# The last expert of each group runs last, and the rows of the first thirty tiles are added to the tokens while it runs

## The chip, the cores and the metric

One core of one Trainium2 chip. The metric is the device time of one execution of the whole program, in microseconds; the runs of a kernel are summed up by their median. The profile is of one further execution.

## The reference

One decoder layer over 1024 tokens of width 1024, all in float32: three kinds of attention side by side, an output projection, and then a mixture of experts. Only the mixture and the final norm matter here:

```python
grp = argmax(h @ w_grp + b_grp)                    # one of 4 groups
top_val, top_idx = top_k(expert logits of grp, 2)  # two of its 8 experts
w_top = softmax(top_val) * grp_gate
for e in range(32):
    out += (silu(h @ w_gate[e]) * (h @ w_up[e]) * gate[:, e]) @ w_down[e]
x = x + out
return rmsnorm(x, norm_final)
```

Each token has exactly two experts, both in one group of eight. So no token has two experts with the same place in a group: experts 7, 15, 23 and 31, the last of the four groups, give each token one row or none.

## The kernel before, in words

The engines run five separate programs that meet at semaphores: SyncE (SP) starts the large DMAs, GpSimd (POOL) the gathers by index, ScalarE (ACT) and VectorE (DVE) compute, TensorE (PE) multiplies. `wait_ge(s, v)` stops the engine that meets it, and all that stands behind it in its program, until semaphore `s` has reached `v`.

The attention comes first and ends near 670 us. The output projection writes `x2`, the residual rows of all tokens, 8 tiles of 128 tokens, in SBUF. The router then sorts the 2048 pairs of token and expert into tiles of at most 96 rows (`CAP`): one tile for each of the 32 experts, and two more (`SURE`) for the experts that have more than 96 tokens. The 34 tiles (`NB`) are run in a loop whose body is written out. I count them 0 to 33 in the order in which they run. For tile n:

- SyncE loads the expert's weights, 2 MB and 1 MB, into one of five sets of buffers (`RING`), when tile n-5's down product is done (lines 728 to 734).
- GpSimd gathers the tile's rows of the normalised input from `h2_d` into `XG` (line 897), one tile or two ahead.
- TensorE transposes them (`m_transposes`, L2144), does the product with the gate and up weights (`m_up`, L2153) and the down product (`m_down`, L2161). Its order is: up n, transposes n+1, down n-1.
- VectorE and ScalarE work out the gate (`m_gate`, lines 1704 to 1717: clamp, exponential on ScalarE, add, reciprocal, two products). In the middle of the gate of tile n VectorE copies its half of the transposed rows of tile n+1 (`m_x`, L1696), without which up n+1 can't start.
- Both copy the result from PSUM (`m_out`, L1723), which the next down product needs, and ScalarE stores 96 rows in `Y_d` in HBM (L1163). VectorE's order is: gate n, copy of n-1.

Experts that overflow further go through a loop of 19 trips (`Fori(0, MAX_OVF - SURE)`), which every engine walks after the 34 tiles; each trip asks `If(j < n_ovf)`. With this input `n_ovf` is 0: the bodies are not run, the loop is walked. Its first step is a load of `n_ovf` into a register (`value_load`).

The last stage starts when both of the last stores have landed: GpSimd gathers for each token tile the first and the second expert's rows of its 128 tokens from `Y_d` into `y1` and `y2` (L921, 16 gathers of 512 KB). VectorE adds each, multiplied by its weight, to `x2` (L1775). ScalarE sums the squares (L1193), and in batches (`K_BATCH`) VectorE refines the inverse roots with five small operations (`k_roots`) and does the final product with the gain (`k_final`, L1769), which SyncE stores (L749). Since every slot of `Y_d` could be read, the rows of unused overflow tiles are zeroed earlier, with seven stores during the attention (L658).

Of the kernel before, what the change touches and what calls it, by code (L numbers as in the profile page):

```python
# [24 lines left out]
P = 128  # L25
# [17 lines left out]
NROWS = NTILES * CAP  # L43
# [157 lines left out]
def program(nc, a, out):  # L201
# [5 lines left out]
    with ctx:  # L207
# [99 lines left out]
        zrow = at("zrow", [P, D // 4], f32, ZE + 32 * KB)  # L307
# [24 lines left out]
        slf, shi, slo = (ri(n, [P, 2, NT]) for n in ("slf", "shi", "slo"))  # L332
# [30 lines left out]
        y1 = at("y1", [P, NT, D], f32, ZD)  # L363
        y2 = at("y2", [P, NT, D], f32, ZD + 32 * KB)
        gfin = at("gfin", [P, D], f32, ZC)
# [10 lines left out]
        Y_d = nc.dram_tensor("Y_d", [NROWS, D], f32).ap()  # L376
# [65 lines left out]
        yz_st = sem("yz_st")  # L442
# [43 lines left out]
        ovf_y = sem("ovf_y")  # L486

# [13 lines left out]
        ZERO = 7  # L501
        ROUTES = ((0, 4, "0"), (4, 6, "1"), (6, 8, "2"))
        A_BATCH = ((0, 1), (1, 1), (2, 2), (4, 4))
        K_BATCH = ((0, 3), (3, 3), (6, 1), (7, 1))

        class Events:
# [8 lines left out]
            def did(self, name, ins, eng=None):  # L515
# [3 lines left out]
                if eng is not None:  # L519
# [13 lines left out]
                       "cj", "ej", "ejc", "nov", "info", "ids_ov"])  # L533
# [18 lines left out]
        def _(sp_):  # L552
# [101 lines left out]
            def zero_rows(i):  # L654

                n0, n1 = (NB + (MAX_OVF - SURE) * j // ZERO for j in (i, i + 1))
                sp_.wait_ge(blk_zero, 3)
                sp_.dma_start(Y_d[n0 * CAP:n1 * CAP, :].rearrange("(p r) (q d) -> p (r q) d", p=CAP, q=4),  # L658
                              zrow[0:CAP].unsqueeze(1).broadcast_to([CAP, 4 * (n1 - n0), D // 4])).then_inc(yz_st, 16)

            stored = 0
            for f, x in enumerate(PLAN.full):
# [12 lines left out]
                if f in range(8, 8 + ZERO):  # L675
                    zero_rows(f - 8)
# [26 lines left out]
            sp_.dma_start(wgu[0][:], a["wgu"][0].rearrange("p (k n) -> p k n", k=KC)).then_inc(we_in[0], 16)  # L703

# [26 lines left out]
            for n in range(NE, NB):  # L731
                eid = sp_.value_load(info[0:1, 1 + n - NE:2 + n - NE], min_val=0, max_val=NE - 1)
                sp_.wait_ge(m_dn, n - RING + 1)
                load_expert(eid, n % RING)
# [12 lines left out]
            for t in range(NT):  # L747
                sp_.wait_ge(k_out, t + 1)
                sp_.dma_start(out[t * P:(t + 1) * P, :], y1[:, t, :]).then_inc(k_st, 16)  # L749
# [6 lines left out]
        def _(pool):  # L756
            pool.sem_inc(m_tr, 2)
            nc.gpsimd.memset(ones[:], 1.0).then_inc(blk_zero, 1)
            nc.gpsimd.memset(zrow[:], 0.0).then_inc(blk_zero, 1)
# [30 lines left out]
            pool.wait_ge(blk_zero, 5)  # L790
# [101 lines left out]
            for n in range(NB):  # L892
                p = n % 2
                pool.wait_ge(m_tr, n + 1)
                if n == NE:
                    pool.wait_ge(dve_did, DV.of("ids_ov"))
                pool.indirect_dma_start(  # L897
                    out=XG[0:CAP, p, :], out_offset=None, in_=h2_d,
                    in_offset=bass.IndirectOffsetOnAxis(ap=ids[0:CAP, n:n + 1], axis=0),
                    bounds_check=SEQ - 1, oob_is_err=False).then_inc(xg_in[p], 16)  # L900
            pool.wait_ge(m_tr, 2 + NB)
            n_ovf = pool.value_load(info[0:1, 0:1], min_val=0, max_val=MAX_OVF - SURE)
            with pool.Fori(0, MAX_OVF - SURE) as j:
                with pool.If(j < n_ovf):
# [7 lines left out]
                        bounds_check=SEQ - 1, oob_is_err=False).then_inc(ovf_x, 16)  # L912

            for p in range(2):
                pool.wait_ge(y_st[p], 16 * NB // 2 + 1)
            pool.wait_ge(yz_st, 16 * ZERO)
            pool.wait_ge(ovf_y, 16 * n_ovf + 1)
            apart(pool)
            for t in range(NT):
# [8 lines left out]
        def _(act):  # L928
# [132 lines left out]
            act.wait_ge(blk_zero, 5)  # L1061
# [94 lines left out]
            def m_out(n):  # L1156
# [6 lines left out]
                act.dma_start(Y_d[n * CAP:(n + 1) * CAP, :], YO[0:CAP, p, :]).then_inc(y_st[p], 16)  # L1163
# [9 lines left out]
            act.wait_ge(yz_st, 16 * ZERO)  # L1173
            act.wait_ge(y_st[0], 16 * NB // 2 + 1)
            n_ovf = act.value_load(info[0:1, 0:1], min_val=0, max_val=MAX_OVF - SURE)
            with act.Fori(0, MAX_OVF - SURE) as j:
                with act.If(j < n_ovf):
# [8 lines left out]
                    act.dma_start(Y_d[ts(j + NB, CAP), :], YO[0:CAP, 0, :]).then_inc(ovf_y, 16)  # L1186
# [13 lines left out]
        def _(dve):  # L1200
# [12 lines left out]
            dve.sem_inc(m_y1, 1)  # L1213
            dve.wait_ge(gbc_in, 16)
# [123 lines left out]
            dve.wait_ge(blk_zero, 5)  # L1338
# [385 lines left out]

            m_x(0)
            overflow_ids()
            for n in range(NB):
                m_gate(n)
                if n:
                    m_out(n - 1)  # L1730
            m_out(NB - 1)
            dve.wait_ge(y_st[0], 16 * NB // 2 + 1)
            n_ovf = dve.value_load(info[0:1, 0:1], min_val=0, max_val=MAX_OVF - SURE)
            with dve.Fori(0, MAX_OVF - SURE) as j:
                with dve.If(j < n_ovf):
# [16 lines left out]
                    V_.tensor_copy(out=YO[0:CAP, 0, 512:D], in_=PS[0:CAP, 6, :]).then_inc(ovf_dve, 1)  # L1752

# [14 lines left out]
            def k_final(t):  # L1768
                V_.scalar_tensor_tensor(out=y1[:, t, :], in0=x2[:, t, :], scalar=rstd[:, t:t + 1],  # L1769
                                        in1=gfin[:], op0=ALU.mult, op1=ALU.mult).then_inc(k_out, 1)  # L1770
# [536 lines left out]
```

## Time and profile before

| what | us |
|---|---|
| median of 3 runs | 1215.21 (1213.35 to 1217.25) |
| span of the profiled execution, first to last instruction | 1207.4 |
| TensorE busy | 1099.9 (91% of the span) |
| VectorE busy | 596.5 (49%) |
| ScalarE busy | 381.1 (32%) |
| GpSimd busy | 211.4 (18%) |
| last matmul ends | 1157.5 |

The profiled execution's own time isn't given beside its span; the median of the three runs lies 7.8 us above that span. Times in the profile are from the span's start. A number behind L is the line of the kernel.

### The profile page before, as it was taken

How to read it: one execution, taken by the hardware profiler on the slowest of the kernel's cores; microseconds unless marked ns; L12 is line 12 of the kernel's file. 1: busy time of each engine (PE TensorE's matmuls, PEld its weight loads, DVE VectorE, ACT ScalarE, POOL GpSimd, SP SyncE). 2: the span in 40 equal slices, each digit the busy share in tenths (PEclk: the TensorE clock that was granted, in tenths of full speed). 3: DMA queues.
4: the chain of work that ended last, by engine and by line, in shares of the span. 5: the costliest groups of instructions: out<-in, count | busy, mean ns of one | idle time of the engine just before them, and what ended most of it. 6: DMA issues, size and time to landing. Idle time of an engine off the chain costs nothing.

```text
span 1207.4 us, 29635 instructions
## 1 busy us (share of the span) xinstructions
PE 1099.9 (91%) x12090; PEld 898.5 (74%) x12090; DVE 596.5 (49%) x1584; ACT 381.1 (32%) x693; POOL 211.4 (18%) x460
## 2 busy tenths in 40 slices
PE   6999899999999999999999899959999999999930
PEld 5989788777788888888777688848777777776710
DVE  5341344224666666665685434474443433333338
ACT  6321112221555555544777122200111111111112
POOL 1030000000523332321484000010110000000031
PEclk9999999999999999999999899968999999999975
DMA  9020755371657887863421422169999999999656
GB/s 356 18 87 16 283 162 157 109 222 70 164 134 198 210 217 186 216 144 81 116 58 26 158 97 96 70 221 360 385 380 373 405 376 374 385 384 370 225 179 267
DMA packets 69431, 251.59 MB, mean 208 GB/s; under 512 B 22225, under 2 KB 30321, under 8 KB 59441
## 3 DMA queue, kind: packets, MB, share of 16 engines
q1 hardware_dynamic: 59376, 219.54, 54.3%
q0 software_dynamic: 6112, 16.79, 4.2%
q10 hardware_dynamic: 3808, 13.37, 2.9%
q8 instruction: 98, 1.61, 0.6%
q14 instruction: 37, 0.30, 0.1%
HBM read 205.34 MB, written 49.15 MB: 211 GB/s over the span
## 4 chain that ended last, share of the span: by engine, by line
PE 75%; DMA 10%; DVE 6%; issue 3%; POOL 2%; ACT 1%; SPq 1%; POOLq 0%; DVEq 0%; ACTq 0%
PE PS L2153 13%; PE PS L1829 12%; PE PS L2007 9%; PE PS L2161 8%; PE PS L2089 7%; PE PS L1818 6%; DMA wdn<-in_wdn 5%; PE PS L1985 4%; PE PS L1946 4%; PE PS L1986 3%; PE PS L2144 2%; DMA wst<-in_wt 1%; DMA k<-T_d 1%; PE PS L1864 1%; PE PS L1979 1%
## 5 line engine op out<-in xcount | busy, mean ns | idle before, releaser
L2153 PEld LDWEIGHTS PS<-XT,wgu 128*64 128x64 f32 x4352 | 185.7, 140 | 33.6 <-issue 32.3
L1090 ACT ACTIVATE pt<-PS,cst 128x512 f32<-128x512 f32 (+3 forms) x288 | 167.2, 650 | 108.5 <-PE PS L1986 82.6
L2153 PE MATMUL PS<-XT,wgu 128*64 128x96 f32 x4352 | 192.2, 250 | 7.6 <-issue 5.1
L1398 DVE CUSTOM_DVE_ANT_0 junkm<-PS,cst 128x512 f32<-128x512 f32 (+3 forms) x276 | 133.5, 531 | 77.5 <-PE PS L1946 75.4
L2007 PEld LDWEIGHTS PS<-V,pt 128*64 128x64 f32 x3840 | 121.7, 138 | 22.5 <-issue 10.4
L2007 PE MATMUL PS<-V,pt 128*64 128x65 f32 x3840 | 137.4, 225 | 0.1
L2161 PE MATMUL PS<-wdn,aT 128*96 128x512 f32 x272 | 122.7, 593 | 1.0 <-DVE YO L1723 0.9
L1829 PE MATMUL PS<-hTh,wth 128*128 128x512 f32 x256 | 102.7, 401 | 4.5 <-DVE wtl L1245 4.5
L1829 PE MATMUL PS<-hTh,wtl 128*128 128x512 f32 x256 | 100.6, 393 | 0.0
L1829 PE MATMUL PS<-hTl,wth 128*128 128x512 f32 x256 | 100.3, 392 | 0.0
L1709 DVE TENSOR_SCALAR ge<-PS 128x192 f32<-128x192 f32 x34 | 12.2, 358 | 164.3 <-PE PS L2153 164.3
L823 POOL TENSOR_SCALAR_AFFINE_SELECT pt<-pt 128x128 f32<-128x128 f32 x224 | 64.2, 292 | 163.2 <-ACT pt L1090 120.8
L897 POOL DMA_INDIRECT XG<-h_d,ids x34 | 32.7, 963 | 296.7 <-PE PS L2144 283.2
L2161 PEld LDWEIGHTS PS<-wdn,aT 128*96 128x96 f32 x272 | 41.7, 163 | 56.4 <-issue 56.3
L1946 PE MATMUL PS<-k,q 128*128 128x128 f32 (+3 forms) x324 | 79.9, 348 | 1.6 <-DMA k<-T_d 1.3
L1985 PE MATMUL PS<-q,k 128*128 128x512 f32 (+1 forms) x228 | 81.2, 370 | 0.0
L1986 PE MATMUL PS<-q,k 65*128 65x512 f32 (+1 forms) x240 | 76.4, 339 | 0.0
L1154 ACT ACTIVATE ge<-ge 128x192 f32<-128x192 f32 x34 | 12.3, 363 | 193.1 <-DVE ge L1709 193.1
L1946 PEld LDWEIGHTS PS<-k,q 128*128 128x128 f32 (+1 forms) x324 | 56.7, 191 | 10.1 <-DMA k<-T_d 1.9
L1829 PEld LDWEIGHTS PS<-hTh,wth 128*128 128x128 f32 x256 | 48.5, 190 | 15.7 <-DVE wtl L1245 5.1
L1829 PEld LDWEIGHTS PS<-hTl,wth 128*128 128x128 f32 x256 | 48.5, 190 | 10.8 <-issue 1.0
L988 ACT ACTIVATE thi<-PS,cst 128x512 fp32r<-128x512 f32 x32 | 21.8, 686 | 109.1 <-PE PS L1829 88.5
(275 smaller groups left out, 1654.8 us busy)
## 6 DMA issues: line engine op xcount, KB each, us to landing
wgu<-in_wgu SPq DMA_DIRECT2D x34, 2048.0 KB, 14.0
wdn<-in_wdn SPq DMA_DIRECT2D x34, 1024.0 KB, 23.7
q<-T_d SPq DMA_DIRECT2D x58, 256.0 KB, 4.3
k<-T_d SPq DMA_DIRECT2D x58, 256.0 KB, 5.4
Y_d<-YO ACTq DMA_DIRECT2D x34, 384.0 KB, 10.1
wst<-in_wt SPq DMA_DIRECT2D x16, 512.0 KB, 6.6
T_d<-thi SPq DMA_DIRECT2D x16, 512.0 KB, 2.6
T_d<-tlo SPq DMA_DIRECT2D x16, 512.0 KB, 3.9
```

The lines of the kernel that those rows point to most:

```text
L823: ins = nc.gpsimd.affine_select(out=o, in_=o, compare_op=ALU.is_ge, fill=0.0, base=0, pattern=[[1, P]], channel_multiplier=-1)
L1090: ins = nc.scalar.activation(pt[:, (n + 2) % 6, 0:nt * P], PS[:, n % 3, 0:nt * P], ACT.Exp, scale=C("slopes", h, h + 1), bias=C("kb", w, w ...
L1398: V_.tensor_tensor_reduce(out=junk_[:, 0:L], in0=PS[:, bank, 0:L], in1=tab, scale=1.0, scalar=-3e38, op0=ALU.add, op1=ALU.max, accum_out=m ...
L1818: ins = mm(o, x[:, k, t * P:(t + 1) * P], wv[w][:, k, :], start=(k == 0 and x is hTh and w == 0), stop=(k == KC - 1 and w == 1))
L1829: ins = mm(PS[:, 2 * p + h, :], w[:, p, k * P:(k + 1) * P], x[:, k, h * 512:(h + 1) * 512], start=(k == 0 and w is wth and x is hTh), stop ...
L1946: ins = mm(PS[:, bank, 0:nk * P], q_[:, t * P:(t + 1) * P], k_[:, k0 * P:(k0 + nk) * P], start=True, stop=True)
L1985: mm(o, k1[:, j * P:(j + 1) * P], q1[:, q], start=True, stop=False)
L1986: ins = mm(o, k2[0:HD + 1, j * P:(j + 1) * P], q2[0:HD + 1, q], start=False, stop=True)
L2007: ins = mm(PS[h * HD:(h + 1) * HD, O_BANK[b % 2], (t % 4) * VW:(t % 4 + 1) * VW], pt[0:rows, (n + 2) % 6, q * P + h * HD:q * P + (h + 1) * ...
L2089: ins = mm(PS[:, 2 + h, :], x[:, t % 2, k, :], w[:, k, h * 512:(h + 1) * 512], start=(k == 0 and x is oth and w is woh), stop=(k == KC - 1 ...
L2153: ins = mm(PS[h * HD:(h + 1) * HD, 2 + p, f * CAP:(f + 1) * CAP], wgu[q][:, c, lo:lo + HD], XT[:, p, c, :], start=(c == 0 and f == 0), sto ...
L2161: ins = mm(PS[0:CAP, 5 + h, :], aT[:, p, c, :], wdn[q][:, c, h * 512:(h + 1) * 512], start=(c == 0), stop=(c == 1))
```

## The change

- `TILE` is a new order: the 28 experts that are not the last of their group, the two overflow tiles, and then experts 7, 15, 23 and 31 (`FINAL`). The first thirty tiles (`EARLY`) are stored in `Y_d`, the last four in `Z_d`. SyncE, GpSimd and ScalarE follow this order.
- After the copy of tile 0 VectorE works out, in `last_rows()`, two sets of weights and of slots: `wa`, `slot_a` for rows that lie in the first thirty tiles, `wf`, `slot_f` for the one row of a token that may lie in the last four. A row that isn't in the set has weight 0 and a slot beyond the bounds, which the gather leaves out.
- Behind its last gather for the tiles, GpSimd waits for the stores up to tile 29 and gathers the 16 sets of early rows into twelve buffers `ye`, which lie over the buffers of tile 29's and tile 30's weights.
- VectorE adds them to `x2`: sets 0 to 2 after the copy of tile 30, sets 3 to 10 after the copy of tile 31, sets 11 to 15 after the copy of tile 33. Each add is followed by a wait for its own completion.
- The last stage gathers one set for each token tile, from `Z_d`, and adds it; the roots come in three batches and not four.
- The walk through the overflow loop stays behind the tiles; on SyncE and VectorE it is now also behind the 16 early adds. Its bodies are longer, because an overflow tile is now added to `x2` inside them.
- The zero stores are gone. The final gain is loaded at the end of the attention. Small tiles lie in the part of the constants that is no longer used.

```diff
+FINAL = tuple(range(7, NE, 8))
+TILE = tuple(e for e in range(NE) if e not in FINAL) + tuple(range(NE, NB)) + FINAL
+EARLY = NB - len(FINAL)
+YROWS = EARLY * CAP
+ZROWS = len(FINAL) * CAP
+SKIP = 2.0 ** 16
...
-        K_BATCH = ((0, 3), (3, 3), (6, 1), (7, 1))
+        K_BATCH = ((0, 3), (3, 3), (6, 2))
...
-                if f in range(8, 8 + ZERO):
-                    zero_rows(f - 8)
...
             sp_.dma_start(wgu[0][:], a["wgu"][0].rearrange("p (k n) -> p k n", k=KC)).then_inc(we_in[0], 16)
+            sp_.dma_start(gfin[:], a["g_fin"]).then_inc(gfin_in, 16)
...
-            for n in range(RING, NE):
+            for n in range(RING, NB):
+                e = TILE[n]
+                if e >= NE:
+                    e = sp_.value_load(info[0:1, 1 + e - NE:2 + e - NE], min_val=0, max_val=NE - 1)
                 sp_.wait_ge(m_dn, n - RING + 1)
-                load_expert(n, n % RING)
...
-            sp_.wait_ge(m_dn, NB - (NB - RING) % RING)
-            sp_.dma_start(gfin[:], a["g_fin"]).then_inc(gfin_in, 16)
+                load_expert(e, n % RING)
             sp_.wait_ge(m_dn, NB)
+            sp_.wait_ge(e_add, 2 * NT)
             n_ovf = sp_.value_load(info[0:1, 0:1], min_val=0, max_val=MAX_OVF - SURE)
...
+            pool.wait_ge(dve_did, DV.of("slot_a"))
+            for p in range(2):
+                pool.wait_ge(y_st[p], 16 * EARLY // 2 + 1)
+            for i in range(2 * NT):
+                if i in (0, 6):
+                    pool.wait_ge(m_dn, EARLY + (i > 0))
+                if i >= 12:
+                    pool.wait_ge(e_add, i - 11)
+                pool.indirect_dma_start(
+                    out=ye[i % 12][:], out_offset=None, in_=Y_d,
+                    in_offset=bass.IndirectOffsetOnAxis(ap=slot_a[:, i % 2, i // 2:i // 2 + 1], axis=0),
+                    bounds_check=YROWS - 1, oob_is_err=False).then_inc(ye_in[i % 12], 16)
...
             for t in range(NT):
-                for k, dst in enumerate((y1, y2)):
-                    pool.indirect_dma_start(
-                        out=dst[:, t, :], out_offset=None, in_=Y_d,
-                        in_offset=bass.IndirectOffsetOnAxis(ap=slot[:, k, t:t + 1], axis=0))\
-                        .then_inc(k_in[t], 16)
+                pool.indirect_dma_start(
+                    out=zt[:, t, :], out_offset=None, in_=Z_d,
+                    in_offset=bass.IndirectOffsetOnAxis(ap=slot_f[:, t:t + 1], axis=0),
+                    bounds_check=ZROWS - 1, oob_is_err=False).then_inc(k_in[t], 16)
...
+            def early_rows(*steps):
+
+                for i in steps:
+                    t, k = i // 2, i % 2
+                    dve.wait_ge(ye_in[i % 12], 16 * (i // 12 + 1))
+                    V_.scalar_tensor_tensor(out=x2[:, t, :], in0=ye[i % 12][:], scalar=wa[:, k, t:t + 1],
+                                            in1=x2[:, t, :], op0=ALU.mult, op1=ALU.add).then_inc(e_add, 1)
+                    dve.wait_ge(e_add, i + 1)
+
             m_x(0)
             overflow_ids()
             for n in range(NB):
                 m_gate(n)
                 if n:
                     m_out(n - 1)
+                if n == 1:
+                    last_rows()
+                if n == EARLY + 1:
+                    early_rows(0, 1, 2)
+                if n == EARLY + 2:
+                    early_rows(*range(3, 11))
             m_out(NB - 1)
+            early_rows(*range(11, 16))
             dve.wait_ge(y_st[0], 16 * NB // 2 + 1)
             n_ovf = dve.value_load(info[0:1, 0:1], min_val=0, max_val=MAX_OVF - SURE)
             with dve.Fori(0, MAX_OVF - SURE) as j:
...
+            dve.wait_ge(ovf_add, 15 * n_ovf + 1)
             for t in range(NT):
-                dve.wait_ge(k_in[t], 32)
-                for k, y in enumerate((y1, y2)):
-                    V_.scalar_tensor_tensor(out=x2[:, t, :], in0=y[:, t, :], scalar=w12[:, k, t:t + 1],
-                                            in1=x2[:, t, :], op0=ALU.mult, op1=ALU.add).then_inc((link, k_acc)[k], 1)
-                    if k == 0:
-                        dve.wait_ge(link, lk.next())
+                dve.wait_ge(k_in[t], 16)
+                V_.scalar_tensor_tensor(out=x2[:, t, :], in0=zt[:, t, :], scalar=wf[:, t:t + 1],
+                                        in1=x2[:, t, :], op0=ALU.mult, op1=ALU.add).then_inc(k_acc, 1)
                 if t == 4:
                     k_roots(0)
-                if t >= 4:
-                    for u in ((0, 1), (2,), (), ())[t - 4]:
-                        k_final(u)
+                if t >= 5:
+                    k_final(t - 5)
             k_roots(1)
-            k_final(3)
+            for t in (3, 4, 5):
+                k_final(t)
             k_roots(2)
-            k_final(4)
-            k_roots(3)
-            for t in (5, 6, 7):
+            for t in (6, 7):
                 k_final(t)
```

## Rows read from the trace of the kernel before

**Rows 1.** The page: its span, and the busy time of each engine.
```profile
span 1207.4 us, 29635 instructions
PE 1099.9 (91%) x12090; PEld 898.5 (74%) x12090; DVE 596.5 (49%) x1584; ACT 381.1 (32%) x693; POOL 211.4 (18%) x460
```

**Rows 2.** Stretches: window, busy us (instructions) by engine, clock, DMA share, GB/s.
```profile
900.00:930.00 30.00, 30.00 (x462) 22.50 (x460) 11.49 (x21) 4.34 (x9) 2.87 (x3) 1.00 1.01 369
...
1135.00:1140.00 5.00, 5.00 (x119) 4.88 (x115) 0.28 (x1) 0.00 (x0) 0.00 (x0) 1.00 0.41 138
```

**Rows 3.** Timeline of the last tiles: start, duration, engine, line, operation.
```profile
1121.94 0.96 POOL L897 DMA_INDIRECT XG<-h_d,ids  x1 [8.72 <-PE PS L2144]
...
1125.38 0.32 ACTq L1163 DMA_DIRECT2D Y_d<-YO  x1
...
1139.72 0.36 DVE L1709 TENSOR_SCALAR ge<-PS 128x192 f32<-128x192 f32 x1 [4.75 <-PE PS L2153]
...
1142.19 0.56 DVE L1696 COPY XT<-PS 128x384 f32<-128x384 f32 x1
...
1143.86 5.50 PE L2153 MATMUL PS<-XT,wgu 128*64 128x96 f32 x128
...
1149.40 0.36 DVE L1709 TENSOR_SCALAR ge<-PS 128x192 f32<-128x192 f32 x1 [4.75 <-PE PS L2153]
...
1153.84 3.64 PE L2161 MATMUL PS<-wdn,aT 128*96 128x512 f32 x8 [0.87 <-DVE YO L1723]
...
1157.52 0.69 DVE L1723 COPY YO<-PS 96x512 f32<-96x512 f32 x1 [3.83 <-PE PS L2161]
```

**Rows 4.** The chain of waits: the first two gathers of the tail.
```profile
1162.28 0.96 POOL y L921
...
1163.54 0.94 POOL y L921
```

**Rows 5.** Timeline of VectorE in the tail.
```profile
1169.30 2.60 DVE L1775 SCALAR_TENSOR_TENSOR x<-y,w,x 128x1024 f32<-128x1024 f32 x2 [11.10 <-DMA y<-Y_d,slot]
...
1172.46 7.64 DVE L1775 SCALAR_TENSOR_TENSOR x<-y,w,x 128x1024 f32<-128x1024 f32 x6 [0.56 <-DMA y<-Y_d,slot]
...
1199.54 0.15 DVE L1760 TENSOR_SCALAR nv<-ssq 128x1 f32<-128x1 f32 x1
...
1200.49 3.68 DVE L1769 SCALAR_TENSOR_TENSOR y<-x,rstd,gfin 128x1024 f32<-128x1024 f32 x3
```

**Rows 6.** Stretches, same columns: among the zero stores, and around 670 us.
```profile
460.00:480.00 20.00, 19.72 (x306) 16.67 (x304) 13.32 (x56) 11.34 (x20) 7.63 (x21) 1.00 0.80 213
...
660.00:680.00 20.00, 15.99 (x149) 13.04 (x149) 9.21 (x25) 5.19 (x12) 3.00 (x12) 0.91 0.58 212
```

**Rows 7.** Stretches, columns as in rows 2: two at low clock, one with a gap.
```profile
671.80:675.10 3.30, 3.15 (x10) 2.69 (x11) 2.96 (x9) 0.99 (x3) 0.00 (x0) 0.51 1.10 444
...
826.50:832.00 5.50, 5.46 (x68) 5.49 (x70) 0.55 (x2) 0.00 (x0) 0.00 (x0) 0.50 1.06 382
...
1105.00:1110.00 5.00, 3.59 (x88) 3.40 (x86) 0.00 (x0) 0.00 (x0) 0.00 (x0) 1.00 0.97 356
```

**Rows 8.** DMA issues at 1125.4, 1121.9 and 1162.3 us; last, us to landing.
```profile
Y_d<-YO ACTq DMA_DIRECT2D x1, 384.0 KB, 8.5
...
XG<-h_d,ids POOLq DMA_INDIRECT x1, 9.4
...
y<-Y_d,slot POOLq DMA_INDIRECT x1, 5.2
```

**Rows 9.** Timeline of TensorE: up product 1.
```profile
826.54 8.14 PE L2153 MATMUL PS<-XT,wgu 128*64 128x96 f32 x128 [2.72 <-issue]
```

**Rows 10.** The overflow loop's instructions: count; ns min/median/max; first and last start.
```profile
L1733 DVEq TENSOR_LOAD <-info x1: 543/543/543, 1157.5 to 1157.5; - x1
...
L1734 DVEq COMPARE_BRANCH  x19: 50/56/66, 1158.9 to 1168.5; - x19
...
L2195 PEldq COMPARE_BRANCH  x19: 214/221/3772, 1159.4 to 1176.5; - x19
```

More of the change, by code:

```diff
@@ L361, in program, with late @@
                for q, o in enumerate((ZE, ZD + 16 * KB, ZD + 40 * KB, ZB + 48 * KB, ZC + 16 * KB))]
-        y1 = at("y1", [P, NT, D], f32, ZD)
-        y2 = at("y2", [P, NT, D], f32, ZD + 32 * KB)
-        gfin = at("gfin", [P, D], f32, ZC)
+        zt = at("zt", [P, NT, D], f32, ZD)
+        ye = [at(f"ye{b}", [P, D], f32, (ZC if b < 6 else ZE) + 4 * KB * (b % 6)) for b in range(12)]
+        dead = (4 * COL["dist"][0] + 31) // 32 * 32
+        gfin = at("gfin", [P, D], f32, dead)
+        _do = [dead + 4 * D]
+        def late(name, shape, dt=f32):
+            n = 4
+            for s in shape[1:]:
+                n *= s
+            t = at(name, shape, dt, _do[0])
+            _do[0] += (n + 31) // 32 * 32
+            assert _do[0] <= 4 * COL["distc"][1]
+            return t
+        lm, am, wa, wl, sf, zf, sd, eq, ew, es = (
+            late(n, [P, 2, NT]) for n in ("lm", "am", "wa", "wl", "sf", "zf", "sd", "eq", "ew", "es"))
+        wf, wd, zs, sj = (late(n, [P, NT]) for n in ("wf", "wd", "zs", "sj"))
+        slf, shi = late("slf", [P, 2, NT]), late("shi", [P, 2, NT])
+        slot_a = late("slot_a", [P, 2, NT], u32)
+        slot_f, slot_j = late("slot_f", [P, NT], u32), late("slot_j", [P, NT], u32)
+        jt = late("jt", [P, 1])
         junk3 = at("junk3", [P, D], f32, ZB + 60 * KB)
@@ L486, in program @@
         ovf_y = sem("ovf_y")
+        ovf_g = sem("ovf_g")
+        ovf_add = sem("ovf_add")
+        ye_in = [sem(f"ye_in{b}") for b in range(12)]
+        e_add = sem("e_add")
         k_in = [sem(f"k_in{t}") for t in range(NT)]
@@ L1752, in _ @@
                     V_.tensor_copy(out=YO[0:CAP, 0, 512:D], in_=PS[0:CAP, 6, :]).then_inc(ovf_dve, 1)
+                    dve.wait_ge(ovf_add, 15 * j + 1)
+                    V_.tensor_scalar(out=eq[:], in0=shi[:], scalar1=jt[:, 0:1], scalar2=None, op0=ALU.is_equal)\
+                      .then_inc(ovf_add, 1)
+                    dve.wait_ge(ovf_add, 15 * j + 2)
+                    V_.tensor_scalar(out=jt[:], in0=jt[:], scalar1=1.0, scalar2=None, op0=ALU.add).then_inc(ovf_add, 1)
+                    V_.tensor_tensor(out=ew[:], in0=eq[:], in1=w12[:], op=ALU.mult).then_inc(ovf_add, 1)
+                    V_.tensor_tensor(out=es[:], in0=eq[:], in1=sd[:], op=ALU.mult).then_inc(ovf_add, 1)
+                    dve.wait_ge(ovf_add, 15 * j + 5)
+                    V_.tensor_tensor(out=wd[:], in0=ew[:, 0], in1=ew[:, 1], op=ALU.add).then_inc(ovf_add, 1)
+                    V_.tensor_tensor(out=sj[:], in0=es[:, 0], in1=es[:, 1], op=ALU.add).then_inc(ovf_add, 1)
+                    dve.wait_ge(ovf_add, 15 * j + 7)
+                    V_.tensor_scalar(out=slot_j[:], in0=sj[:], scalar1=SKIP, scalar2=None, op0=ALU.add)\
+                      .then_inc(ovf_add, 1)
+                    dve.wait_ge(ovf_g, 16 * NT * j + 16 * NT)
+                    for t in range(NT):
+                        V_.scalar_tensor_tensor(out=x2[:, t, :], in0=zt[:, t, :], scalar=wd[:, t:t + 1],
+                                                in1=x2[:, t, :], op0=ALU.mult, op1=ALU.add).then_inc(ovf_add, 1)
             dve.wait_ge(gfin_in, 16)
```

94 lines of the change are left out of this document (64 added, 30 removed).

## The prediction

> **What bounds the kernel now.** I read the page first: a span of 1207.4 us with TensorE busy in 91% of it and VectorE in half [rows 1]. The stretches say which stage the change touches. From 830 to 1157 us the 34 expert tiles run; TensorE is busy without a gap and the DMA engines are full too, at 369 GB/s; from 1130 us on the last expert weights drain and the DMA share falls to 0.41 [rows 2]. One tile takes 9.68 us (1139.72 to 1149.40, the gate's first operation in two tiles [rows 3]). In the tail the chain of waits goes from the last copy over its store to GpSimd's gathers, the first at 1162.28 [rows 4], and from 1169.3 VectorE sets the pace: 16 adds and 8 final products of 1.28 us each, with small groups of root operations between [rows 5]. So there are two things to price: what happens from 1125 to 1157 us, where TensorE is the bound, and what VectorE does in series after it. The profiled span is 7.8 us under the median of the runs shown (1215.21); I add the same 7.8 us to the new span.
>
> **Parts that cost nothing.** The seven zero stores leave a stretch where TensorE is busy 19.72 of 20 us and DMA 0.80 of its time [rows 6]; nothing there waits for them: 0, at best the 0.28 us of idle. The load of the final gain moves from 1124.6 us to 670 us, 0.5 MB behind the first expert's weights in a window with a DMA share of 0.58 [rows 6]: 0, up to 2 us if the next load of attention output waits behind it. `last_rows()` adds 22 small operations on VectorE after the copy of tile 0. A small one takes 0.16 us and 0.2 with its link (five in the 0.95 us from 1199.54 to 1200.49 [rows 5]), so 4.4 us; VectorE is idle for 4.75 us before each gate [rows 3], that of tile 2 too. Hidden, by 0.3 us; if not, the gate has 1.1 us in hand (below). The two nearly empty overflow tiles now run 29th and 30th of the 34 and four full experts last: about 0.5 MB of gathered rows moves from the DMA-bound part to behind it. TensorE lost 1.41 us there (busy 3.59 of 5 [rows 7]). I credit 0.5 us (bounds 0 and 1.4).
>
> **The early gathers hold VectorE, and VectorE holds TensorE.** GpSimd starts the 16 early gathers when the store of tile 29 has landed. That store is issued at 1125.38 and takes 8.5 us: 1133.9 [rows 3, 8]. GpSimd needs 0.8 us from a release to its gather (released by the transposes' end at 1121.13, start 1121.94 [rows 3]): 1134.7. The starts are 1.25 us apart (1162.28, 1163.54 [rows 4]); the third is at 1137.2. Landing: 5.2 us on idle DMA engines, 9.4 us among weights [rows 8]; with 0.41 of the DMA time in use [rows 2] I take the middle, 7.3 us: 1144.5. VectorE adds rows 0, 1, 2 between tile 30's copy and tile 32's gate (each add 1.28), so that gate starts at 1145.8 and not at 1139.72: 6.1 us late.
>
> Queued behind it: tile 32's gate contains the copy of tile 33's X. That ended at 1142.75 and its reader, up product 33, started at 1143.86 [rows 3], a slack of 1.1 us. Up product 33 now starts at 1145.8 + 3.0 + 0.15 = 1149.0, 5.1 us late, with TensorE idle in between.
>
> The gate ends at 1145.8 + 3.7 = 1149.5, tile 31's copy adds 0.7: 1150.2. Then eight more adds stand before tile 33's gate; six took 7.64 us [rows 5], eight take 10.2: 1160.4 (their rows are in; the eleventh gather starts at 1147.2). Up product 33 is done by 1157.2 even if it takes 8.14 us [rows 9], so the adds come last. The gate takes 3.2 us without a copy of X, tile 32's copy 0.7, and the last down product waits for that copy, as it does now [rows 3]: start at 1160.4 + 3.2 + 0.7 + 0.15 = 1164.5, where it was 1153.84: 10.7 us late. TensorE has by then been idle for 4 us or more.
>
> **The clock.** After 2.72 us idle TensorE came back at 0.50 (1.2 GHz) and kept it for 5.5 us of work: up product 1 took 8.14 us where up product 33 took 5.50 [rows 3, 7, 9]. Elsewhere the low clock lasted 3.3 us (671.8 to 675.1), and 1.41 us idle cost none [rows 7]. So the last down product, 3.64 us at full clock [rows 3], starts at the low one: 5.3 us if that lasts 3.3, 7.3 if it lasts throughout. I take 6.2: it ends at 1170.7, where it was 1157.5.
>
> **The tail.** Copy 0.7: 1171.4. VectorE adds rows 11 to 15, 5 x 1.28 = 6.4 (their gathers are long in): 1177.8. Now comes what the old profile hides. Each engine loads the number of overflow tiles and walks an empty loop of 19 trips. On VectorE that runs from 1157.5 to 1168.55, 11.05 us [rows 10], beside the store and the first gathers, and its first add came at 1169.3. In the new program each early add ends in a wait that stops the sequencer, so the loop starts at 1177.8 and ends at 1188.9. SyncE's loop waits for the same adds, but the first output store is needed only some 8 us later. GpSimd walks its loop from about 1156, before the last store lands. The gathers of the last stage start 4.8 us after the last product, as now (1157.5 to 1162.28 [rows 3, 4]): 1175.5; the first lands by 1180.7, the eighth (start 1184.3) by 1189.5. All of that is hidden behind the loop. That only about an eighth of the rows is fetched (4 of 32 experts) gains nothing here.
>
> From 1188.9 VectorE has 8 adds and 8 final products, 16 x 1.28 = 20.5, and three groups of roots of 1.0 us: 23.5, so 1212.4. The last final product ended at 1204.17 and the span at 1207.4, 3.25 later [rows 1, 5]: 1215.7.
>
> **Sum.** The last product is 13.2 us late. From its end to the span's end it was 49.9 us and is now 0.7 + 6.4 + 11.05 + 23.5 + 3.25 = 44.9: the eight adds and the root group that go are worth 11 us, but five early adds and the uncovered loop take more than half of that back. 13.2 - 5.0 = 8.2, less 0.5 for the order of tiles: 7.8 us slower, rounded. Span 1215.2, time 1223.0.
>
> **Rules weighed.** Rows 8 show a gather of unchanged form taking 9.4 us among weights and 5.2 alone. The Trainium skill (DMA: Bandwidth & Descriptors, "Queues, rings and completion order") says that a DMA engine takes turns among the queues that have work for it. By that rule a gather shares evenly on every engine that still has weights, and gather 2 would land nearer to 9.4: 2 us more in the sum.
>
> Rows 10 show the first skip over TensorE's long loop body taking 3772 ns. The Trainium skill (Runtime: NRT & Kernel Launch, "Instruction fetch mechanics") says that a taken branch to code outside the pages at hand waits for a fetch. The new loop bodies of VectorE and GpSimd are several times as long as the old ones, which makes a rival.
>
> **Rivals.**
> *The adds come free* (faster). VectorE is idle 4.75 us before each gate [rows 3]. If the rows land before 1140 and the eight adds go into idle time, TensorE ends at 1157.5 as now and only the tail counts: 5.0 us faster, 1210.2. For it: the DMA engines are half free from 1130. Against it: the store of tile 29 alone lands at 1133.9, and eight adds are 10.2 us, twice the idle time. It decides if the gate of tile 33 starts by 1150.
>
> *The loop is not in series* (no change). If VectorE's sequencer walks the empty loop under the adds, the first late add starts when its row lands, 1180.7, and the end is 1180.7 + 23.5 + 3.25 = 1207.4: 1215 us. For it: the register load started at 1157.5, before the copy on the same engine had ended at 1158.2 [rows 3, 10]. Against it: each early add has a wait on its own completion behind it.
>
> *Longer loop bodies stall on code* (slower still). One such stall of 3.8 us gives 1227; one in every other trip of a few tenths, as much again, gives 1230.
>
> **How the numbers follow.** Forecast 0.62; longer bodies 0.10; loop not in series 0.13; adds free 0.15. The forecast's own range: landing of gather 2 from 5.2 to 10.5 us (-2.1, +3.2), the store of tile 29 up to 1 us sooner, the last down product -0.9 to +1.1, order of tiles -0.9 to +0.5, the moved load up to +2: 1218 to 1230. The whole range goes on one side most of the way to 1210.2 and on the other past 1230: 1211 to 1232. A measurement here tells about 0.3% (3.6 us) from no change. Below 1211.6 lies the one faster case; the loop case and the lowest end of the forecast are "same": faster 0.15, same 0.16, slower 0.69.
>
> **What would show it.** VectorE: three adds that wait for gathers before tile 32's gate, eight in a row between tile 31's copy and tile 33's gate. TensorE: idle about 5 us before up product 33 and 4 us or more before the last down product, with a granted clock of 0.5 in both. After the five last early adds an interval of 11 us in which VectorE's queue shows only moves and branches while the gathered rows are already there. The forecast is wrong if the last product ends before 1163, or if the first late add follows the last early one by less than 5 us.

## The result, and the profile after

The changed kernel took 1218.43 us in the median of 20 runs (1214.77 to 1228.67). The kernel before took 1213.52 us in 20 runs on the same chip (1206.75 to 1217.25). The ratio is 1.0057, with a 95% interval of 1.0039 to 1.0075: By that ratio the change costs 6.9 us (4.7 to 9.1), where 7.8 had been forecast; the two medians themselves lie 4.9 us apart. The rows in this section are those of one profiled execution of each kernel.

The head of the page after, against [rows 1]:

```profile
span 1217.9 us, 29701 instructions
PE 1105.4 (91%) x12090; PEld 902.0 (74%) x12090; DVE 609.4 (50%) x1609; ACT 380.2 (31%) x691; POOL 220.9 (18%) x467
```

The span grew by 10.5 us. TensorE has the same number of matmuls and is busy for 5.5 us longer; VectorE has 12.9 us more work.

The timeline of GpSimd and VectorE after (start, duration, engine, line, operation, and in brackets the idle time before it and what ended that). It answers to [rows 3, 5].

```profile
1137.85 1.01 POOL L929 DMA_INDIRECT ye<-Y_d,slot_a  x1 [12.68 <-PE PS L2268]
...
1140.47 0.99 POOL L929 DMA_INDIRECT ye<-Y_d,slot_a  x1 [0.30 <-issue]
...
1178.87 1.93 POOL L961 DMA_INDIRECT zt<-Z_d,slot_f  x1 [18.44 <-issue]
```

```profile
1126.88 0.69 DVE L1767 COPY YO<-PS 96x512 f32<-96x512 f32 x1 [0.56 <-PE PS L2268]
...
1146.13 3.98 DVE L1808 SCALAR_TENSOR_TENSOR x<-ye,wa,x 128x1024 f32<-128x1024 f32 x3 [8.35 <-DMA ye<-Y_d,slot_a]
1150.14 0.36 DVE L1753 TENSOR_SCALAR ge<-PS 128x192 f32<-128x192 f32 x1
...
1154.34 10.52 DVE L1808 SCALAR_TENSOR_TENSOR x<-ye,wa,x 128x1024 f32<-128x1024 f32 x8
1164.89 0.36 DVE L1753 TENSOR_SCALAR ge<-PS 128x192 f32<-128x192 f32 x1
...
1174.10 0.69 DVE L1767 COPY YO<-PS 96x512 f32<-96x512 f32 x1 [5.41 <-PE PS L2268]
1174.71 6.55 DVE L1808 SCALAR_TENSOR_TENSOR x<-ye,wa,x 128x1024 f32<-128x1024 f32 x5
1192.52 6.07 DVE L1886 SCALAR_TENSOR_TENSOR x<-zt,wf,x 128x1024 f32<-128x1024 f32 x5 [11.26 <-issue]
...
1212.25 2.48 DVE L1880 SCALAR_TENSOR_TENSOR zt<-x,rstd,gfin 128x1024 f32<-128x1024 f32 x2
```

The reader sees the forecast order of things: three adds that end a wait for a gather, right ahead of tile 32's gate; eight in a row and then tile 33's gate; five after the last copy; and then 11.26 us in which VectorE waits for nothing that the profile shows, although the first late gather started at 1178.87 and landed 4.0 us later.

One releaser in these rows is misleading. The profile infers that TensorE's down product of tile 30, which ended at 1137.06, released the first early gather at 1137.85. The store of tile 29, issued at 1127.7 and 9.3 us on its way, landed at 1137.0 as well. In the eight traces in which the gathers weren't held back, the first one starts 9.95 to 10.3 us after that store is issued, but anywhere from 0.2 to 1.1 us after the down product. So it is the store, as forecast.

TensorE after, same columns:

```profile
1143.14 3.60 PE L2268 MATMUL PS<-wdn,aT 128*96 128x512 f32 x8
1153.27 7.95 PE L2260 MATMUL PS<-XT,wgu 128*64 128x96 f32 x128 [6.53 <-issue]
1161.15 3.67 PE L2268 MATMUL PS<-wdn,aT 128*96 128x512 f32 x8
1168.84 5.22 PE L2268 MATMUL PS<-wdn,aT 128*96 128x512 f32 x8 [4.01 <-DVE YO L1767]
```

And the stretches there (busy us of PE, PEld, DVE, ACT and POOL, granted clock, DMA share, GB/s):

```profile
1145.00:1150.00 5.00, 1.74 (x5) 0.35 (x3) 3.75 (x3) 0.00 (x0) 3.78 (x5) 1.00 1.01 407
1150.00:1155.00 5.00, 1.73 (x22) 1.76 (x24) 4.43 (x9) 1.22 (x3) 4.09 (x4) 0.65 1.01 370
1155.00:1160.00 5.00, 5.00 (x86) 5.00 (x85) 4.86 (x5) 0.00 (x0) 4.08 (x4) 0.66 0.94 338
...
1165.00:1170.00 5.00, 1.16 (x2) 0.62 (x3) 3.16 (x6) 0.84 (x2) 0.00 (x0) 0.86 0.10 28
```

TensorE is idle for 6.53 and 4.01 us. After the first gap the granted clock is 0.50 until 1158.3 (1.2 GHz, the lower of its two levels), which shows as 0.65 and 0.66 in two stretches, and up product 33 takes 7.95 us instead of 5.50. The sixteen gathers fill the DMA engines (1.01, where [rows 2] have 0.41 with only the last weights on their way).

The overflow loop's instructions on VectorE's queue after (count; ns min/median/max; first and last start), against [rows 10]:

```profile
L1827 DVEq TENSOR_LOAD <-info x1: 552/552/552, 1181.3 to 1181.3; - x1
...
L1828 DVEq COMPARE_BRANCH  x19: 50/56/66, 1182.7 to 1192.3; - x19
```

The same instructions at the same durations, but the load now starts at 1181.3, when the last early add has ended, and the last branch comes just ahead of the first late add. The DMA issues, for those made from 1137.5 to 1141 us and at 1127.7 us (KB each, us to landing), against [rows 8]:

```profile
ye<-Y_d,slot_a POOLq DMA_INDIRECT x3, 8.2
...
Y_d<-YO ACTq DMA_DIRECT2D x1, 384.0 KB, 9.3
```

### The profile page after: what moved, and what is told of

It reads as the page before. It is cut to its first block, busy times and chain, and to the rows that moved or that the text cites. A ratio compares the mean times of both kernels' runs of the same rounds, so it can differ in the third digit from the quotient of the medians.

```text
span 1217.9 us, 29701 instructions
## 1 busy us (share of the span) xinstructions
PE 1105.4 (91%) x12090; PEld 902.0 (74%) x12090; DVE 609.4 (50%) x1609; ACT 380.2 (31%) x691; POOL 220.9 (18%) x467
## 4 chain that ended last, share of the span: by engine, by line
PE 73%; DMA 10%; DVE 8%; issue 4%; ACT 1%; POOL 1%; SPq 1%; DVEq 1%; POOLq 0%; ACTq 0%
PE PS L1936 12%; PE PS L2260 12%; PE PS L2114 9%; PE PS L2268 8%; PE PS L2196 7%; PE PS L1925 5%; DMA wdn<-in_wdn 5%; PE PS L2092 4%; PE PS L2053 4%; PE PS L2093 3%; PE PS L2251 2%; DVE x L1808 2%; DMA wst<-in_wt 1%; PE PS L1971 1%; DMA k<-T_d 1%
## 5 line engine op out<-in xcount | busy, mean ns | idle before, releaser
L2268 PE MATMUL PS<-wdn,aT 128*96 128x512 f32 x272 | 125.8, 606 | 4.0 <-DVE YO L1767 4.0
L1936 PEld LDWEIGHTS PS<-hTh,wtl 128*128 128x128 f32 x256 | 48.5, 189 | 10.4
```

What stands on the lines that cost most here:

```text
L1936: ins = mm(PS[:, 2 * p + h, :], w[:, p, k * P:(k + 1) * P], x[:, k, h * 512:(h + 1) * 512], start=(k == 0 and w is wth and x is hTh), stop ...
L2268: ins = mm(PS[0:CAP, 5 + h, :], aT[:, p, c, :], wdn[q][:, c, h * 512:(h + 1) * 512], start=(c == 0), stop=(c == 1))
```

## Experiments

Each kernel was compared with the kernel before on its own chip, and the chips differ. The kernel before took 1212 us on chip 0, 1218 to 1219 on chips 2 and 3, and 1222 on chip 11. Which chip ran the first comparison is not recorded; by its times (1213.5 and 1.0057) and its trace it behaved as chip 0 does. So ratios are compared, and the chip is named with each.

| run | edit | chip | median us | ratio to before [95%] |
|---|---|---|---|---|
| a_guard | changed kernel, VectorE's loop guarded | 3 | 1222.4 | 1.0036 [1.0019, 1.0053] |
| b_guard | kernel before, same guard | 3 | 1209.48 | 0.9932 [0.9914, 0.9951] |
| a_late | changed kernel, all early adds last | 3 | 1234.07 | 1.0141 [1.0110, 1.0173] |
| a_late_guard | both | 3 | 1229.2 | 1.0097 [1.0078, 1.0116] |
| a_same | changed kernel as it is | 0 | 1217.8 | 1.0047 [1.0028, 1.0067] |
| b_same | kernel before as it is | 0 | 1210.55 | 0.9989 [0.9967, 1.0010] |
| a_held | a_late, early gathers held back | 0 | 1218.7 | 1.0051 [1.0031, 1.0071] |
| a_fit_guard | guard, adds in other places | 0 | 1200.84 | 0.9906 [0.9873, 0.9939] |
| a_guard2 | as a_guard | 2 | 1223.23 | 1.0036 [1.0019, 1.0053] |
| b_guard2 | as b_guard | 2 | 1212.49 | 0.9940 [0.9923, 0.9958] |
| a_same2 | changed kernel as it is | 11 | 1239.82 | 1.0141 [1.0112, 1.0170] |
| b_same2 | kernel before as it is | 11 | 1222.43 | 1.0004 [0.9986, 1.0022] |

### The loop skipped: a_guard and b_guard

If VectorE's empty loop stands in series in the changed kernel alone, a jump over it must pay there and not in the kernel before. I call that jump the guard. The same edit was made in both kernels, on VectorE only; `n_ovf` is 0 in this data, so what is computed stays whole.

```
 n_ovf = dve.value_load(...)
-with dve.Fori(0, MAX_OVF - SURE) as j:
-    with dve.If(j < n_ovf):
+with dve.If(n_ovf > 0):
+    with dve.Fori(0, MAX_OVF - SURE) as j:
+        with dve.If(j < n_ovf):
```

> The changed kernel, with VectorE's empty loop of 19 trips behind one question: is the number of overflow tiles above 0. Nothing else differs. My theory: the loop stands in series behind the early adds (last one ends 1181.3, first late add starts 1192.5) while the first gathered rows landed at 1182.9, so the first late add comes some 9 us sooner and the end too: about 1209 us, 0.997 of before. Rival, the late end of TensorE is what costs: the end does not move, 1218 us.

> The kernel before with the same one question in front of VectorE's loop. My theory: there the loop (1157.5 to 1168.55) ran beside the store and the first gathers, whose rows landed at 1169.2, so nothing is gained: 0 to 0.7 us, ratio 1.000. Rival, 19 empty trips cost their 10 us wherever they stand: 1203 us, ratio 0.992.

Measured: 1.0036 and 0.9932. VectorE's timeline in a_guard:

```profile
1145.73 3.95 DVE L1808 SCALAR_TENSOR_TENSOR x<-ye,wa,x 128x1024 f32<-128x1024 f32 x3 [8.58 <-issue]
1159.59 0.36 DVE L1753 TENSOR_SCALAR ge<-PS 128x192 f32<-128x192 f32 x1 [9.91 <-PE PS L2261]
...
1187.06 6.55 DVE L1808 SCALAR_TENSOR_TENSOR x<-ye,wa,x 128x1024 f32<-128x1024 f32 x5
1196.08 4.87 DVE L1887 SCALAR_TENSOR_TENSOR x<-zt,wf,x 128x1024 f32<-128x1024 f32 x4 [2.47 <-issue]
```

The part of the theory that the guard tests held: the wait ahead of the first late add is 2.47 us and not 11.26. But the ratio does not show it, because something else had gone wrong before: tile 32's gate starts 9.91 us after the adds, and what it waited for was TensorE. In b_guard the expectation of no change was a miss. The guard was worth 0.7% there, and neither surprise could be explained from these two runs alone.

### All early adds last: a_late and a_late_guard

If the three and eight adds ahead of the gates are what delays TensorE, TensorE must keep its pace when they go behind the last copy.

```
-                if n == EARLY + 1:
-                    early_rows(0, 1, 2)
-                if n == EARLY + 2:
-                    early_rows(*range(3, 11))
             m_out(NB - 1)
-            early_rows(*range(11, 16))
+            early_rows(*range(16))
```

> The changed kernel with all 16 early adds behind the copy of tile 33; none stands among the tiles. Both theories expect TensorE without its two gaps and the last product some 14 us earlier, at 1160. My theory, VectorE's work in series sets the end: copy ends 1160.5, 16 adds of 1.31 us end at 1181.5, where the changed kernel has 1181.3, then loop and late adds as now: 1218 us, within 1.5 us of the changed kernel. Rival, the delay of TensorE is the cost: 14 us faster, 1204.

> Both edits together: all early adds behind the last copy, and the question in front of VectorE's loop. My theory: early adds end at 1181.5, rows of the last stage have landed by then, so the end is that of the kernel with the question alone, about 1208 us, and about 10 us under the one with late adds alone. Rival, delay of TensorE: 1204 or less, the loop adding nothing.

Measured: 1.0141 and 1.0097. As a test of TensorE's delay both failed, since up product 32 went wrong here too (below). The tails can still be read. VectorE in a_late, then in a_late_guard:

```profile
1174.15 21.08 DVE L1808 SCALAR_TENSOR_TENSOR x<-ye,wa,x 128x1024 f32<-128x1024 f32 x16
1207.05 6.07 DVE L1882 SCALAR_TENSOR_TENSOR x<-zt,wf,x 128x1024 f32<-128x1024 f32 x5 [11.81 <-issue]
```

```profile
1175.13 21.08 DVE L1808 SCALAR_TENSOR_TENSOR x<-ye,wa,x 128x1024 f32<-128x1024 f32 x16
1197.55 6.11 DVE L1883 SCALAR_TENSOR_TENSOR x<-zt,wf,x 128x1024 f32<-128x1024 f32 x5 [1.34 <-issue]
```

Two kernels that differ in the guard alone, on one chip: it takes 10.5 us out of the wait (11.81 to 1.34), and the profiled spans differ by 9.5 us (1232.4, 1222.9). The medians differ by 4.9 us only; a_late's six runs spread over 11.3 us. The 1218 us expected of a_late was missed by 16, since TensorE did not end at 1160 but at 1173.5.

### The pair unchanged on chip 0, and the gathers held: a_same, b_same, a_held

a_same and b_same are the two kernels without an edit, to have the change measured beside the next kernels. a_held is a_late with one more line, so that no early gather runs beside an up product:

```
             for p in range(2):
                 pool.wait_ge(y_st[p], 16 * EARLY // 2 + 1)
+            pool.wait_ge(m_gu, NB)
```

> The changed kernel, unchanged, to have its trace and its ratio on the chip of the runs beside it. In three kernels that differ from it only on VectorE, TensorE lost 12 to 17 us inside up product 32, whose matmuls came a few at a time about 0.7 us apart, from the moment the early gathers filled the DMA engines. If that is tied to those kernels, this one runs up product 32 in 5.5 us and has the ratio of 1.006. If it is a thing of chance or of the chip that gathers bring about, it shows here too and the ratio is up to 1.012.

> The kernel before, unchanged. The one question in front of VectorE's loop made it 8 us faster where its trace lets only 1 us go. If the loop is the reason, this trace shows a first add in the tail well behind the landing of its rows. If TensorE's starts and stops among full DMA engines are, it shows more gaps without a releaser in the expert tiles than the one with the question (there 3 us), and the tail is alike. Ratio 1.000.

> All early adds behind the last copy, and the early gathers besides held until the last up product is done, so that no gather runs beside the up products 32 and 33. Theory, the gathers slow TensorE inside up product 32 by filling the DMA engines: this kernel has up product 32 in 5.5 us, the last product ends near 1160, the rows land at about 1.3 us intervals from 1159 on, VectorE ends its 16 adds at 1182 and walks its loop until 1193: 1217 to 1220 us, 14 us under the one with late adds alone (1.014). Rival, the slow up product has nothing to do with the gathers: it is slow here too, 1232 us.

Measured: 1.0047, 0.9989 and 1.0051. The timeline of a_held, TensorE and then VectorE:

```profile
1135.60 5.50 PE L2257 MATMUL PS<-XT,wgu 128*64 128x96 f32 x128
...
1155.25 3.65 PE L2265 MATMUL PS<-wdn,aT 128*96 128x512 f32 x8 [0.87 <-DVE YO L1768]
```

```profile
1158.93 0.69 DVE L1768 COPY YO<-PS 96x512 f32<-96x512 f32 x1 [3.83 <-PE PS L2265]
...
1166.03 15.91 DVE L1809 SCALAR_TENSOR_TENSOR x<-ye,wa,x 128x1024 f32<-128x1024 f32 x12 [0.75 <-DMA ye<-Y_d,slot_a]
1193.19 6.07 DVE L1883 SCALAR_TENSOR_TENSOR x<-zt,wf,x 128x1024 f32<-128x1024 f32 x5 [11.25 <-issue]
```

This run says what the delay on TensorE is worth. Here TensorE ends its last product at 1158.9, where a_same on the same chip has 1173.2, and the time is the same (1.0051 and 1.0047). What TensorE no longer loses, VectorE has to do afterwards: all 16 adds, the loop and 22 us of late adds and final products stand behind the copy. The held gathers cost the adds 1.3 us of waiting (0.54 and 0.75) in that time, not more. So between these two placements nothing is won: the end is set by VectorE's serial work, since the eleven adds ahead of the gates take 14.5 us off the end and TensorE ends 14.3 us later for them. As a test of the slow up product this run decides nothing, since a_same on the same chip doesn't show it either.

### The version that follows: a_fit_guard

Guard in, and the adds placed where VectorE is idle and TensorE has slack: three after tile 31's copy, two after tile 32's, eleven after the last.

```
-                if n == EARLY + 1:
-                    early_rows(0, 1, 2)
                 if n == EARLY + 2:
-                    early_rows(*range(3, 11))
+                    early_rows(0, 1, 2)
+                if n == EARLY + 3:
+                    early_rows(3, 4)
             m_out(NB - 1)
-            early_rows(*range(11, 16))
+            early_rows(*range(5, 16))
```

> The changed kernel with the question in front of VectorE's loop and the early adds where VectorE is idle: rows 0 to 2 behind the copy of tile 31, 3 and 4 behind that of tile 32, the other 11 behind the last copy. If TensorE keeps its pace the last product ends at 1160, 11 adds end at 1175, 23.5 us of VectorE and 3.2 follow: span 1202 us, ratio 0.995. If the gathers slow up product 32 here as well, 12 to 15 us more: 1215 us, 1.006.

Measured: 0.9906 (0.995 expected), faster than both kernels: 11.4 us under the kernel before and 17 under the changed one on that chip. Its timeline, TensorE and then VectorE:

```profile
1148.13 5.50 PE L2261 MATMUL PS<-XT,wgu 128*64 128x96 f32 x128
...
1158.10 3.65 PE L2269 MATMUL PS<-wdn,aT 128*96 128x512 f32 x8 [0.87 <-DVE YO L1767]
```

```profile
1148.84 3.91 DVE L1808 SCALAR_TENSOR_TENSOR x<-ye,wa,x 128x1024 f32<-128x1024 f32 x3
1153.75 0.36 DVE L1753 TENSOR_SCALAR ge<-PS 128x192 f32<-128x192 f32 x1 [0.99 <-PE PS L2261]
...
1162.45 14.48 DVE L1808 SCALAR_TENSOR_TENSOR x<-ye,wa,x 128x1024 f32<-128x1024 f32 x11
1178.26 6.10 DVE L1887 SCALAR_TENSOR_TENSOR x<-zt,wf,x 128x1024 f32<-128x1024 f32 x5 [1.34 <-issue]
```

TensorE loses nothing: the last down product starts after a gap of 0.87 us, as in [rows 3]. From its end (1161.8) to the span's end (1203.7) it is 41.9 us, where the kernel before has 49.9. Those 8 us are seen in the trace; the median gained 11.4, with an interval of 7.4 to 15.4. The spans of the profiled executions don't show the gain (1203.7, and 1204.9 in b_same) because these two differ ahead of the tail: the copy of tile 29 starts at 1128.57 in this one and at 1121.41 in b_same, and the one was among the slower of its six runs, the other among the quicker of its twelve. The guard alone was not run on chip 0, so how the gain splits between guard and places is not measured.

### Repeats on other chips: a_guard2, b_guard2, a_same2, b_same2

Two questions were open: is the slow up product the guard's doing or the chip's, and why does the guard help the kernel before?

> The changed kernel with the question in front of VectorE's loop, once more, since the first time its up product 32 ran slowly among the gathers and covered what the tail gained. On the chip where the changed kernel and the one with moved adds ran at pace: if the slow up product belongs to the other chip, up product 32 takes 5.5 us, the first late add follows the last early one within 2 us and the ratio is about 0.998 (0.8% under the changed kernel). If it belongs to this kernel, its ratio is 1.004 again and up product 32 takes about 20 us.

> The kernel before with the question in front of VectorE's loop, once more: the first time its ratio was 0.993 where the two traces (from two chips) differ by 1 us in the tail. My theory from the traces, that the loop was covered: 1.000, at best 0.999. Rival, the walk costs 8 us on VectorE before as well: 0.993 again.

> The changed kernel, unchanged, once more. In all four kernels whose up product 32 was slow among the gathers the chip was another than that of the changed kernel's traces. If it is the chip, the changed kernel has the slow up product there as well, a ratio near 1.012, and the question in front of the loop (1.0036 on two such chips) was worth 10 us as my theory has it. If it is those kernels, up product 32 takes 5.5 us here and the ratio is 1.005; the same ratio on the first chip again would leave it open.

> The kernel before, unchanged, once more, for its trace on a chip where the question in front of the loop made it 0.6% faster. If the walk of the loop is longer there among the full DMA engines, VectorE's first add comes some 6 to 8 us after its rows have landed; if not, it comes within 1 us as in the trace at hand and the 0.6% lies ahead of the tail. Ratio 1.000.

Measured: 1.0036 and 0.9940 on chip 2, the values of chip 3 again; 1.0141 and 1.0004 on chip 11. The two pairs ran on different chips. a_guard2 had been meant for the chip of the changed kernel's first trace and came to another, so its question stayed open until a_same2. TensorE's timeline in a_same2, which is the changed kernel without an edit:

```profile
1137.41 3.73 PE L2260 MATMUL PS<-XT,wgu 128*64 128x96 f32 x79
1141.45 0.39 PE L2260 MATMUL PS<-XT,wgu 128*64 128x96 f32 x4 [0.31 <-issue]
...
1142.97 0.39 PE L2260 MATMUL PS<-XT,wgu 128*64 128x96 f32 x3 [0.30 <-issue]
```

Stretches of the same run:

```profile
1137.00:1142.00 5.00, 4.53 (x85) 3.71 (x84) 0.69 (x1) 0.59 (x1) 2.79 (x3) 1.00 0.67 220
...
1147.00:1152.00 5.00, 2.57 (x12) 1.02 (x11) 3.31 (x3) 0.00 (x0) 3.78 (x5) 0.50 0.98 354
```

From the moment at which the early gathers fill the DMA engines, TensorE issues a handful of matmuls, then stands still, and goes on 0.7 us (later also 1.4 or 2.1 us) after it last began; in the gaps it waits for nothing that the profile shows. Up product 32 lasts until the gate at 1160.80, 23 us instead of 5.5. Rows of the same kind stand in a_guard, a_guard2, a_late and a_late_guard (chips 3 and 2), and in neither a_same (chip 0) nor the changed kernel's first trace. So it is not the guard's doing. That it is the chip's and not chance of an execution is likely: all five runs of a_same2 took 1237 to 1241 us, all twelve of a_same 1214 to 1222. On chip 11 the change costs 1.41%, 18 us, instead of 0.5%. Against a_same2's 1.0141 the guard's 1.0036 is a gain of about 1%, 13 us; the wait ahead of the first late add is 15.62 us in a_same2 and 2.47 in a_guard, which is 13 us too. That comparison crosses chips.

The kernel before on the same chip 11 (b_same2), VectorE's loop and its first add:

```profile
L1734 DVEq MOVE  x20: 9/36/724, 1162.5 to 1182.6; - x20
...
L1734 DVEq COMPARE_BRANCH  x19: 14/56/700, 1162.9 to 1186.8; - x19
```

```profile
1186.17 12.67 DVE L1775 SCALAR_TENSOR_TENSOR x<-y,w,x 128x1024 f32<-128x1024 f32 x10 [23.94 <-issue]
```

The empty loop lasts until 1186, 24 us instead of 10, with single moves and branches of up to 0.7 us; ten adds then run back to back, since their rows have long been in (the first gather started at 1166.30). On this chip the loop is in series in the kernel before as well. From the last product's end to the span's end it is 61.6 us here, 49.9 in the trace of the kernel before, and 50.0 and 49.8 in b_guard and b_guard2. So the guard brings the tail on chips 3 and 2 to the length that it has on chip 0 without one, and a stretched loop is its likely cause of gain there. It isn't shown: the kernel before was not profiled without a guard on chips 2 and 3. In a_late on chip 3, the one unguarded loop there, the branches took at most 66 ns, beside the eight late gathers and a DMA share of 0.24; in a_same2 on chip 11, beside the same gathers and 0.23, they took up to 706 ns.

## Why the prediction was right

Tail and middle went by the forecast mechanism, and both signs by which it was to be called wrong stayed away: the last product ended at 1174.1 and not before 1163, and the first late add came 11.26 us after the last early one. That the sum came within 1 us is in part luck. Net of what the two executions differ by ahead of the change's own steps (2.3 us, next paragraph), the last product ended 14.3 us late where 13.2 were forecast, and the tail behind it was 6.1 us shorter where 5.0 were forecast: two errors of 1.1 us that cancel. The first of them is itself a remainder, of 2.0 us too little for the gathers and 1.0 too much for the clock.

**The base.** Of the 10.5 us between the spans, 2.3 were there before the first early gather: the copy of tile 29 starts that much later than before (1126.88, where it was 1124.61). 2.8 us had been lost by the first output product already (669.37, where it was 666.59). I had allowed up to 2 us for the moved load of the final gain, but that load is issued only at 673.10, so it is not the reason. Executions differ at this point: 663.57 in b_same, and 670.08, 668.38 and 670.82 in a_same, a_held and a_fit_guard. The changed kernels are all later than the kernel before, so a part may be the change's own; no run separates it. The other 8.2 us of the 10.5 are the steps that I had forecast at 8.2, before the 0.5 taken off for the order of tiles. The 7.8 us by which I raised the base were not a constant: a run's time stands only about 1.8 us over its span (1219.65 and 1217.9 in the execution profiled after), and the rest was that the profiled execution of the kernel before came from the quick end of its spread (an estimate from that 1.8: 1209.2 us, and only three of the 20 runs were quicker). With 1.8 the forecast time would have been 1217.0 and not 1223.0; 1218.43 was measured. The step did no harm to the forecast difference, but it is not what I said it was.

**The early gathers.** Store of tile 29: 9.3 us, not 8.5. Landing of gather 2: 8.2 us, not 7.3, since the gathers themselves fill the DMA engines: from 1141 to 1148 us their queue alone takes 0.91 of the engines' time; the middle between 5.2 and 9.4 leaned the wrong way. Net of the 2.3 us, tile 32's gate came 8.1 us late (forecast 6.1), up product 33 7.1 (5.1), tile 33's gate 13.2 (11.0), the last down product 12.7 (10.7). So all links behind the gathers held to 0.2 us, and the two DMA terms with GpSimd's small ones were 2 us short.

**The clock.** Up product 33 took 7.95 us, partly at the low level, which cost nothing, as forecast: the adds came last. The last down product took 5.22 us, not 6.2: the granted clock was 0.50 for its first 3 us and then full, which is the shorter of the two cases that I had averaged (5.3 us). In a_guard it took 6.43 us after an idle time of 6.12, so the average was not out of reach.

**The tail.** 43.8 us from the last product's end, forecast 44.9. The five adds took 6.55 us (6.4), the interval 11.26 (11.05), the rest 22.2 (23.5): adds and final products start 1.20 us apart and not 1.28, which the three final products in 3.68 us of [rows 5] had shown. The late gathers were hidden behind the loop, as forecast. The guard shows the loop term itself: 1.34 us in its place in a_late_guard.

**The order of tiles** was credited with 0.5 us. From the first output product to tile 29's copy the kernel before took 458.0 and 457.8 us (in its trace and b_same), the changed one 457.5, 455.5, 456.6 and 457.8 (its trace, a_same, a_held, a_fit_guard). The 0.5 fits these numbers, but it wasn't tried alone. The prediction says of these tiles both that TensorE is busy without a gap and that it lost 1.41 us; the gap in [rows 7] is there, so the second is right.

**The rivals.** *Adds come free* fell by the gates at 1150.14 and 1164.89. a_fit_guard shows that part of it can be had: five adds do go into idle time if they stand where it is. *Loop not in series* fell by the 11.26 us and by the guard. *Longer bodies stall* fell by the rows after, where the branches took 50 to 66 ns as before; on chip 11 branches did stall, up to 0.7 us, but in the short loops of the kernel before too (24 us there, some 15 in a_same2), so length is not what does it. *Longer bodies* is refuted only for loops whose bodies are not run.

What I missed altogether is that on some chips TensorE itself slows inside an up product from the moment the early gathers run. It had no row in the trace of the kernel before, where one gather comes in a tile, and it is not in the first result. As a statement on chip 11 the forecast of 0.6% would have been wrong by a factor of two.

## What to carry to other kernels

Work moved out of the tail must go where its engine is idle and nothing waits behind it; on an engine that works in order, adds ahead of a gate delay TensorE by what reaches past the moment at which the gate could have started. Here the eight adds ended at 1164.9, where up product 33 had ended at 1161.2, and the three and their wait ended at 1150.1, where up product 32 had ended at 1142.5. a_held shows that putting them all last is no better. Look in a profile for control flow that hides under a wait: on chip 0 an empty loop of 19 trips cost nothing until the work around it was shortened, and one branch around it took 10.5 us out of the wait. Measure a change on more than one chip before trusting half a per cent.

## What the runs showed of the hardware

The slow up product is open. It appears on chips 2, 3 and 11 in five traces, and not on chip 0; DMA load alone doesn't make it, for a_fit_guard runs an up product in 5.50 us beside gathers on chip 0:

```profile
1148.00:1153.50 5.50, 5.50 (x129) 5.31 (x128) 4.45 (x4) 0.59 (x1) 4.58 (x4) 1.00 1.03 385
```

The Trainium skill (Runtime: NRT & Kernel Launch, "Instruction fetch mechanics") says that each engine's sequencer fetches its next page of instructions by a DMA queue of its own. The page of a_same2 shows such packets: 98 on queue q8 and 37 on q14, of kind instruction. A fetch that comes too late behind 16 gathers would give gaps with no releaser, in TensorE's matmuls as in VectorE's loop, and the steps of 0.7 us in both suggest one cause. But the trace of a_same2 speaks against such a fetch. From 1146 to 1166 us, while TensorE stops and goes until 1160.6, no packet of kind instruction moves at all:

```profile
DMA packets 1728, 5.60 MB, mean 280 GB/s; under 512 B 362, under 2 KB 362, under 8 KB 1728
q0 software_dynamic: 1728, 5.60, 74.3%
```

The same holds in a_guard from 1142 to 1166, in a_guard2 from 1146 to 1170, and in b_same2 from 1170 to 1186, in the stretched loop. From a late page I would expect one long gap that ends with a packet, and not seventeen short gaps, most of them without any. So the cause stays open. That the gathers bring it about is argued from the moment at which it begins. What would test that, the gathers held on a chip that has the slow product, wasn't run; nor was a_fit_guard there.

A compare-and-branch takes 56 ns in the median on VectorE here, and 221 on TensorE's queue [rows 10]. The Trainium skill (Advanced Engine Details and Errata, "Control Flow Timing") gives about 108 without naming an engine, and the other queues don't have that number either: it is 45 ns on those of SyncE, ScalarE and GpSimd in the trace after.
